# Hybrid encoder on one core: the first expert's tokens chosen by comparing every token with every other, and the first expert's work in a new order

## What is computed

```
def expert_choice_ffn(h, w_router, w_exp_gate, w_exp_up, w_exp_down):
    aff = jax.nn.softmax((tok @ w_router).astype(jnp.float32), axis=-1)
    cap = EC_CAPACITY_FACTOR * N // N_EXPERTS
    gate, idx = lax.top_k(aff.T, cap)
    xs = tok[idx]
    hid = jax.nn.silu(jnp.einsum('ecd,edf->ecf', xs, w_exp_gate)) * jnp.einsum('ecd,edf->ecf', xs, w_exp_up)
    out = jnp.einsum('ecf,efd->ecd', hid, w_exp_down) * gate[..., None].astype(h.dtype)
    y = jnp.zeros((N, D), out.dtype).at[idx.reshape(-1)].add(out.reshape(-1, D))
```

## Time and profile before

| | us |
|---|---|
| median of 3 executions (2385.63 to 2387.28) | 2386.59 |
| the profiled execution's own time | 2386.68 |
| its span in the trace | 2384.8 |
| TensorE busy in the span | 2360.4 |
| VectorE busy | 1624.6 |
| ScalarE busy | 1488.6 |
| GpSimd busy | 401.4 |

### The profile page before, as it was taken

One profiled execution on the slowest core, in us unless ns is written; L12 is line 12 of the kernel. 1 busy time (PEld: TensorE's weight loads), 2 busy tenths in 40 slices (PEclk: granted clock), 3 DMA queues, 4 the chain that ended last, 5 costly groups with the idle time before them and its releaser, 6 DMA issues.

```text
span 2384.8 us, 33778 instructions
## 1 busy us (share of the span) xinstructions
PE 2360.4 (99%) x11804; PEld 1967.3 (82%) x11804; DVE 1624.6 (68%) x1767; ACT 1488.6 (62%) x1707; POOL 401.4 (17%) x279
## 2 busy tenths in 40 slices
PE   8999999999999999999998999999999999999998
PEld 7888888888888888888885888888888888888886
DVE  5545464634546455455346988888888888888897
ACT  5656564533466465554335777777777777777776
POOL 1533433000053324320002000000000000000000
PEclk9999999999999999999999999999999999999999
DMA  6413321125432224112238999999999999999998
GB/s 189 128 45 100 88 73 67 70 98 204 158 98 83 83 62 126 64 63 80 90 155 334 403 393 382 383 383 381 390 387 393 387 383 383 385 387 376 394 375 326
DMA packets 214395, 557.35 MB, mean 234 GB/s; under 512 B 11968, under 2 KB 93376, under 8 KB 209216
## 3 DMA queue, kind: packets, MB, share of 16 engines
q1 hardware_dynamic: 207280, 530.89, 60.4%
q0 software_dynamic: 7056, 25.69, 3.6%
HBM read 533.47 MB, written 23.07 MB: 233 GB/s over the span
## 4 chain that ended last, share of the span: by engine, by line
PE 97%; DVE 1%; DMA 0%; issue 0%; ACT 0%; POOLq 0%; SPq 0%; DVEq 0%; ACTq 0%
PE bank L1433 44%; PE bank L1073 15%; PE bank L1118 13%; PE bank L1039 7%; PE bank L1062 5%; PE bank L1093 3%; PE bank L1236 2%; PE bank L1479 2%; PE bank L1134 2%; PE bank L1217 1%; PE bank L1156 1%; PE bank L1197 1%; PE bank L1203 1%; PE bank L1160 1%; PE bank L1252 0%
## 5 line engine op out<-in xcount | busy, mean ns | idle before, releaser
L2575 DVE TENSOR_TENSOR m_lo<-m_raw,m_hi 128x2048 fp32r<-128x2048 f32 x380 | 867.4, 2290 | 121.0 <-ACT m_hi L1925 117.4
L1925 ACT ACTIVATE m_hi<-m_raw 128x2048 fp32r<-128x2048 f32 x382 | 733.6, 1921 | 261.5 <-PE bank L1433 256.6
L1433 PE MATMUL bank<-m_hi,xs_hi 128*128 128x512 f32 x1032 | 321.0, 392 | 0.0
L1433 PE MATMUL bank<-m_hi,xs_lo 128*128 128x512 f32 x1032 | 317.9, 389 | 0.0
L1433 PE MATMUL bank<-m_lo,xs_hi 128*128 128x512 f32 x1032 | 317.8, 389 | 0.0
L2063 DVE TENSOR_TENSOR w_lo<-w_raw,w_hi 128x1152 fp32r<-128x1152 f32 (+4 forms) x110 | 145.0, 1344 | 180.1 <-ACT w_hi L1561 180.0
L1433 PEld LDWEIGHTS bank<-m_lo,xs_hi 128*128 128x128 f32 x1032 | 193.7, 188 | 40.5
L1433 PEld LDWEIGHTS bank<-m_hi,xs_lo 128*128 128x128 f32 x1032 | 193.7, 188 | 40.4
L1433 PEld LDWEIGHTS bank<-m_hi,xs_hi 128*128 128x128 f32 x1032 | 191.4, 188 | 38.2 <-DVE xs_lo L2597 0.2
L1073 PE MATMUL bank<-h_hi,w_hi 128*128 128x512 f32 x512 | 203.0, 396 | 0.0
L1073 PE MATMUL bank<-h_lo,w_hi 128*128 128x512 f32 x512 | 199.6, 390 | 0.0
(11 more groups left out here) (292 smaller groups left out, 4239.4 us busy)
## 6 DMA issues: line engine op xcount, KB each, us to landing
m_raw<-in_w_exp_gate SPq DMA_DIRECT2D x128, 1024.0 KB, 8.1
m_raw<-in_w_exp_up SPq DMA_DIRECT2D x128, 1024.0 KB, 7.6
m_raw<-in_w_exp_down SPq DMA_DIRECT2D x128, 1024.0 KB, 7.4
w_raw<-in_w_b SPq DMA_DIRECT2D x66, 512.0 KB, 6.2
w_raw<-in_w_a SPq DMA_DIRECT2D x24, 1024.0 KB, 5.1
w_raw<-in_w_c SPq DMA_DIRECT2D x24, 1024.0 KB, 4.8
w_raw<-in_w_d SPq DMA_DIRECT2D x8, 1024.0 KB, 6.5
xt<-in_x SPq DMA_DIRECT2D x8, 512.0 KB, 7.9
```

The costliest lines, as they stand in the source:

```text
L1433: mm = pe.matmul(ps[:, half, :], a[:, chunk + k, :], v[:, k, 512 * half:512 * (half + 1)], start=first and k == n == 0, stop=last and k == ...
L1925: act.activation(m_hi[slot.slot][:, :, :], m_raw[raw.slot][:, :, :], ACT.Copy)\
L2575: dve.tensor_tensor(m_lo[slot.slot][:, :, :], m_raw[raw.slot][:, :, :], m_hi[slot.slot][:, :, :].bitcast(F32), ALU.subtract)\
```

## The change

**First expert.** Only expert 0's slots are needed to begin. For it, VectorE counts for each token how many tokens of its group have a higher affinity. The affinities, multiplied by 2 to the 64 (`raised`), are spread over all partitions by four transposes on TensorE (`t`), four comparisons on VectorE of 512, 384, 256 and 128 columns (`r`, `compared`) write a mark for each pair and the sum of each row, six matmuls of three columns (`c`) count the pairs not compared, and a subtraction and two comparisons of 256 columns (`o`) mark which token belongs in which slot. Twelve one-column matmuls (`q`) turn the marks into the index and the affinity of each slot; `p` writes them out. For the first group all of this stands inside the closing part: `h` and `t` after the third `D`, `r` after the fourth, `c` and `o` after the fifth. A table of constants (`rank_table`, 784 columns) is loaded for it.

**All other experts.** The eight rounds remain, split into three, three and two: the first three after the index is written, the next three after the `m_lo` of unit 10, the last two and the merge after that of unit 15. Their lists are turned by TensorE ahead of unit 16 (`lists_turned`).

**Weights.** SP waits ahead of unit 2, rather than ahead of unit 7, until the gather has landed and the picks are done. `final_gain` is loaded after unit 15 instead of ahead of unit 0. GpSimd splits units 0, 12 and 16 (`POOLED`).

**First expert's order.** Gate and up of both halves come first (units 0 to 15), then the eight down units; the hidden rows of the second half are turned between units 18 and 19, and the rows of expert 1 between units 22 and 23. Unit 24 on are gate and up of expert 1's first half. In the kernel before, units 16 to 19 are down, 20 to 27 are expert 1's gate and up, 28 to 31 down; from unit 32 both have one order. The loop over experts has one turn less. The matmuls that nobody reads between rounds go, and those ahead of the gathered rows are three calls instead of six.

```diff
+POOLED = (0, 12, 16)
...
+        if last and i == NT - 2:
+            out += [("h", 0), *(("t", 0, i) for i in range(NT))]
+    if last:
+        out += [("r", 0, j) for j in range(NT)]
+    out += [("D", 1, 0), *((("c", 0), ("o", 0)) if last else ()), ("Y", 0), *ahead[NT:NT + 1], ("M", 0), ("D", 1, 1), ("Y", 1), *ahead[NT + 1:], ("N", 0),
...
-                if unit.k == RAW_SLOTS - 1:
+                if unit.k == 2:
 
                     sp.wait_ge(s_gather, 16)
+                    sp.wait_ge(s_picked, 2 * NB)
...
+            for n, k in enumerate(POOLED):
+                raw, cut = k % RAW_SLOTS, k % SPLIT_SLOTS
+                pool.wait_ge(s_mhi, k + 1)
+                pool.wait_ge(s_rounds, n + 1)
+                pool.tensor_tensor(m_lo[cut][:, :, :], m_raw[raw][:, :, :], m_hi[cut][:, :, :].bitcast(F32),
+                                   ALU.subtract).then_inc(s_plo, 1)
...
+                elif what == "t":
+
+                    of = arg[0]
+                    if i == 0:
+                        all_read(pe, s_out_free, outs)
+                        all_read(pe, s_proj_free, proj, but=0 if of else 2)
+                    pe.wait_ge(s_raised, of * (1 + i) + 1)
+                    pe.transpose(ranked[of][:, natural(i)], raised[:, of, i:i + 1].to_broadcast([P, P]), ident[:, :])\
+                        .then_inc(s_rows, 1)
...
-            for k, times in enumerate(WARM_ROUNDS.values()):
-                pe.wait_ge(s_round, k + 1)
-                keep_busy(times, ps_proj[:, 0, :])
...
+            def compared(of, nth):
+
+                j, cols = NT - 1 - nth, P * (NT - nth)
...
+                dve.scalar_tensor_tensor(beats[j][:, :], ranked[of][:, 0:cols], raised[:, of, j:j + 1], margins[:, T - cols:],
+                                         ALU.subtract, ALU.is_gt, accum_out=row_sum[:, of, j:j + 1]).then_inc(s_beats, 1)
...
+            dve.sem_inc(s_rounds, 1)
+            eight_best(0)
+            eight_best(1)
+            eight_best(2)
+            split_unless_pooled()
+            transposed_lo(xs_hi, xs_lo)
+            split_units(3)
+            after()
+            split_units(4)
+            after()
+            split_units(2)
+            hidden_step()
+            split_units(1)
+            dve.sem_inc(s_rounds, 1)
+            eight_best(3)
+            eight_best(4)
+            eight_best(5)
+            split_units(1)
+            after()
+            split_unless_pooled()
+            split_units(2)
+            transposed_lo(hid_hi, hid_lo)
+            split_units(1)
+            after()
+            dve.sem_inc(s_rounds, 1)
+            eight_best(6)
+            eight_best(7)
+            halves_merged()
+            split_unless_pooled()
+            routes()
+            split_units(1)
+            hidden_step()
+            split_units(2)
+            after()
+            split_units(1)
+            transposed_lo(hid_hi, hid_lo)
```

More of the change, by code:

```diff
@@ L440, in hybrid_encoder @@
         part_sums = [a[:, k, P:2 * P] for a in (ps_sc, ps_out) for k in range(2)]
+        ranked = [ps_out[:, 1, :], ps_proj[:, 1, :]]
+        counts = [ps_sc[:, 0, 256 + 4 * b:256 + 4 * b + NT - 1] for b in range(NB)]
+        pick = ps_sc[:, 1, 256:257]
+        pick_gate = ps_sc[:, 0, 272:273]
         ps_g, ps_t, ps_u, ps_d = bank
@@ L602, in tile_read, with lo_ready @@
             eng.wait_ge(s_proj_free[proj.slot], START + proj.lap + 1)
+        def lo_ready(eng, unit, behind=0):
+            k = unit.k - behind
+            if k in POOLED:
+                eng.wait_ge(s_plo, POOLED.index(k) + 1)
+            else:
+                eng.wait_ge(s_mlo, unit.n(1 - behind - sum(each < k for each in POOLED)))
         def all_stored(eng, count):
@@ L944, in _ @@
                     seam_step(what, arg, b)
-            for i in range(EARLY_SPLITS):
-                pool.wait_ge(s_mhi, i + 1)
-                pool.tensor_tensor(m_lo[i][:, :, :], m_raw[i][:, :, :], m_hi[i][:, :, :].bitcast(F32),
-                                   ALU.subtract).then_inc(s_mlo, 1)
             all_stored(pool, NB)
@@ L990, in _ @@
             gather(1, 1)
-            with pool.Fori(0, NE - 2) as e:
+            pool.wait_ge(s_mtr, 8)
+            pool.wait_ge(s_gather, 32)
+            gather(2, 2)
+            add(0, 3)
+            with pool.Fori(1, NE - 2) as e:
                 pool.wait_ge(s_mtr, e * 6 + 6)
@@ L1534, in _ @@
             up_cols()
-            with rolled(pe, NE - 1, mt, {"unit": 24, "slot": 24, "tr": 6, "step": 2}) as e:
-                expert(e, False)
+            gate_cols()
+            hidden_transposes(1)
+            up_cols()
+            operand_ready()
+            lists_turned()
+            for j in range(4):
+                use(ps_d, hid_hi, hid_lo, MK * j, j == 0, False)
+                if j == 2:
+                    hidden_transposes(2)
+            operand_ready(1)
+            for j in range(4):
+                if j == 2:
+                    operand_ready()
+                use(ps_d, hid_hi, hid_lo, MK * j, False, j == 3)
+                if j == 2:
+                    token_transposes(32)
+            operand_ready()
+            gate_cols()
+            up_cols()
+            with rolled(pe, NE - 2, mt, {"unit": 24, "slot": 24, "tr": 6, "step": 2}) as e:
+                expert(e, False, shift=1)
             expert(NE - 1, True)
@@ L2039, in _ @@
             per = {"raw": 24, "slot": 24, "unit": 24, "done": 24, "tr": 6, "step": 2}
-            with rolled(act, NE - 1, mt, per) as e:
-                expert(e)
+            with rolled(act, NE - 2, mt, per) as e:
+                expert(e + 1)
             last_expert()
@@ L2532, in _, with eight_best @@
             all_read(dve, s_tr_free, tr)
-            for r in range(CAP // 8):
+            def eight_best(r):
                 eight = slice(8 * r, 8 * r + 8)
```

246 lines of the change are left out of this document (181 added, 65 removed), and 3 rows, old and new, of the table out.

## The result

The changed kernel takes 2393.36 us (median of 12 runs, 2391.39 to 2394.85); the kernel before took 2386.56 us beside it (12 runs). The ratio is 1.0028, 95% interval 1.0021 to 1.0035: slower, 6.8 us by the medians. The loss is over the 4.8 us (0.2%) that the prediction called no change, so it is the slower outcome, which had 22%, and not the one within, which had 64%. The profiled execution took 2393.32 us around a span of 2391.3, against 2384.8 before: 6.5 us more.

What follows compares the result with a forecast made beforehand. The prediction took TensorE's queue of matmuls to bound the kernel, with lack of work only ahead of the experts. Terms -8.2 + 1.6 + 2.1 + 3.5 + 3.3 = +2.3 us gave 2389.0 us, range 2381.5 to 2393.5.

Steps and rivals of the forecast that it cites:

- the five places named: Waits of TensorE forecast ahead of units 2, 11, 17, 18 and 20, the longest ahead of 11.
- rival B: First expert's start: TensorE at half speed in units 0 and 1, 3.8 us added, 2392.8 us; 12%.
- rival A: Expert 0: the lead survives as stocks build up before unit 11; -5.6 us, 2381.1 us; 14%.
- lead: Start of expert 0: index 10.2 us sooner, less 2.0 for the closing part, so 8.2 us sooner.
- unit 2: Expert 0: unit 2, asked for when the gather has landed, comes late; +1.6 us, bounds 1 and 4.
- units 3 to 9: Expert 0: loads trail and units come just in time; +2.1 us, bounds 0 and 4.
- unit 11: Expert 0: three rounds and hidden rows on VectorE ahead of unit 11's split; +3.5 us, bounds 1.8 and 5.
- rest of expert 0: List transposes and waits ahead of units 17, 18 and 20; +3.3 us, bounds 1.5 and 5.
- The closing part: Between the projections: 1.05 us of TensorE standstill, transposes 0.5 and six three-column matmuls 0.4; sum +2.0 us.
- GpSimd's 1 us and the gather's 5.05 stay: Behind the index: the gather's start and landing take as long as before; rows land at 1276.3.
- rival C: Gather: waits for its source, the last normalised tile, landing 1.4 us behind the index; 2390.4 us; 6%.
- the forecast case: Whole kernel: the lead is real and the first expert gives it back; +2.3 us, 2389.0 us; 68%.

Runs made afterwards that it cites:

- e3_pool0: Changed kernel with GpSimd splitting unit 0 only, the splits of units 12 and 16 back on VectorE: 2394.09 us.
- e4_rounds5: Changed kernel with GpSimd splitting unit 0 only and VectorE's rounds moved: five ahead of the gathered rows, one ahead of unit 11's split: 2388.72 us.
- e10_pooled: Best kernel (parts together, SyncE's wait ahead of unit 4) with the splits of units 12 and 16 given to GpSimd again: 2388.77 us.
- e9_warm5: Best kernel (parts together, SyncE's wait ahead of unit 4) with five calls of warming matmuls ahead of the rows instead of three: 2383.96 us.
- e1_gate3: Changed kernel with SyncE's wait for the gather ahead of unit 3 instead of unit 2: 2391.51 us.
- experiments 1 and 3: Changed kernel: 1, gather wait ahead of unit 3 or 7, 2391.51 and 2395.07 us; 3, rounds moved, GpSimd splitting unit 0 only, 2388.72 us.
- Experiment 2: Changed kernel with GpSimd's two later splits (units 12 and 16) back on VectorE: 2394.09 us.

## Why the prediction was right or wrong

The cause was right: the index comes early, and the first expert gives the lead back at the five places named. The size was not: the loss was 6.5 us where 2.3 were forecast, and the upper end of the range, which held it by 0.1 us, had been set for rival B, which did not come. That is luck. (Its lower end, 2381.5, is not quite rival A's own sum, 2381.1.) In the prediction's own terms (end of unit 31):

| term | forecast | measured | what failed |
|---|---|---|---|
| lead | -8.2 | -7.3 | the gather waited for its source |
| unit 2 | +1.6 | +4.1 | wait 2.6, lost clock 1.5 |
| units 3 to 9 | +2.1 | 0 | no wait |
| unit 11 | +3.5 | +5.9 | wait 4.25, lost clock 1.7 |
| rest of expert 0 | +3.3 | +3.5 | right by chance |
| start after the two long waits | 0 | +0.3 | not in the waits, which count from the modelled end of the matmul before |

**The closing part** was 1.02 us of standstill as worked out (1.05), and 2.4 us in all, by the last residual addition (1258.41 instead of 1256.02), instead of 2.0. The four comparisons took 0.75 to 0.35 us, the marking 0.38 each: the index came within 0.2 us of the forecast time.

**"GpSimd's 1 us and the gather's 5.05 stay"** failed. The gather started 2.2 us behind the index and its rows took 4.5 us, 0.7 us more in sum; with the index 0.2 us late, the rows came 0.9 us after the forecast time. GpSimd's queue waits for the stores first, and the last normalised tile, stored at 1262.52, took 9.1 us to land, at 1271.6; the gather followed 1.1 us later. The issue of that store is in the rows above; its landing, from the DMA issues between 1256 and 1272 (KB, us from issue to landing):

```profile
normed<-norm POOLq DMA_DIRECT2D x1, 512.0 KB, 9.1
```

In the profiles of the changed kernel and the twelve made from it the gather starts 10.1 to 11.4 us behind that store's issue, wherever the index is (2.0 to 3.5 us ahead of the gather), and always 1.0 to 1.1 us behind the store's landing. This is rival C, which had 6% and 1.4 us; it added 1.2 us beside the forecast case instead of taking its place. Its sum was wrong too: a landing at 1272.7 is 2.4 us behind the index of 1270.3 that the same prediction gives, not 1.4. The landing came 1.1 us sooner than that. The Trainium skill's rule of turns between the queues (DMA: Bandwidth & Descriptors, Queues, rings and completion order) gave, by the prediction's estimate, a landing within about 5 us. It took 9.1 us; the row with 10.6 was the better guide, and the small chance given to rival C was the error.

**Unit 2, "a 1 MB load takes 4.8 us with little beside it"**: there was not little. Six loads start together, and unit 2 reached ScalarE 6.5 us behind the rows. The wait of 2.6 us is inside the bounds of 1 to 4. What stood in no term is the clock. Rival B asked only whether TensorE starts at half speed; it did not. The falls came later and cost 1.5 and 1.7 us behind the waits ahead of units 2 and 11; this is the largest thing that the sum lacked. The prediction had said that waits there could cost clock, and gave it no number. The Trainium skill (TensorE: Matmul & The Clock Gate, What's actually happening) has what is issued after idleness run at 1.2 GHz, half speed, and the two stretches agree; but not every such wait does it: after 2.50 us in e3_pool0 and e4_rounds5 and 3.45 us in e10_pooled the clock stayed at 1.00, while it fell after 2.60 us here and 3.33 us in e3_pool0. The length of the wait alone does not tell, so the theory of e9_warm5, that every wait of over two microseconds costs clock, does not hold. What decides it is open.

**Units 3 to 9, "just in time: +2.1"**: no wait. ScalarE did wait for DMA at units 3 to 7, 1.06 us and then some 0.65 each, one unit every 2.56 us, but unit 2's 4.1 us had given the loads that much room. Where unit 2's wait is gone (e1_gate3), unit 8 waits 0.70 us. Two terms priced the same lateness.

**Unit 11, "three rounds ahead of its split: +3.5"**: the wait was 4.25. VectorE's order makes it, as forecast (experiments 1 and 3), within 1.8 to 5. Of the 2.4 us above the forecast 1.7 is the lost clock, and in the wait itself 1.3 us is the split of unit 11 held up by GpSimd's split of unit 12, which the prediction took as work done elsewhere for nothing. Experiment 2 takes it away and the wait is 3.33 us.

**The rest** fitted: from the first transposes of hidden rows to the mark 60.8 us pass instead of 57.3. That is more than the waits, 1.9 us (0.5 ahead of units 17 and 18, where 1.1 was forecast, and 1.4 ahead of unit 20, where it was 1.9), and the list transposes, 0.3; behind each stop the pairs of matmuls start some tenths late. It fitted by chance: the prediction counted 2.3 us back from GpSimd's split of unit 16, and the copy, held for 2.25 us, took most of that away.

## What to carry to other kernels

A transfer or a result that comes earlier is worth only what the queues behind it can keep up: count the stock (here two loads instead of seven) and place the displaced work where its engine idles, not ahead of the next operand. Price a wait of TensorE like these, of 2.4 to 4.6 us, at its length plus up to 2.4 us of half-speed matmuls (1.5 and 1.7 in the changed kernel, 2.4 in e1_gate3, nothing after 2.50 us in two kernels and 3.45 us in a third). And work handed to GpSimd isn't off VectorE's back where both read their operands from SBUF: they go one behind the other, and an operation of 2.3 us can be held for as long as GpSimd's 4.5 us last.

## What the runs showed of the hardware

- In the splits and the copy here, GpSimd and VectorE exclude each other for whole instructions: a VectorE split of 2.28 us took 6.51 us, a 64x64 copy 2.25 us instead of 0.19, GpSimd's split 6.70 us instead of 4.5. MAX8, FIND_INDEX8 and MATCH_REPLACE8 kept their 0.41 to 0.43 us.
- A comparison with row sums costs a read of its own, DVE_READ_ACCUMULATOR, but only 0.08 us.
- A GpSimd gather of 128 rows took 4.5 us with few loads in flight and 8.1 us beside five more; a GpSimd store of 512 KB took 9.1 to 10.6 us beside weight loads, and 2.9 us where no weight load ran (the earlier tiles in the kernel before).
- The same loop ran at 67.96 or 68.06 us per expert with different programs around it, and at the same pace when one program was run again. What decides it is open.
